# Two transformer blocks of each of two kinds on one core: rotary step of the windowed queries moved to GpSimd, maxima negated in the reduction, attention steps reordered

## The reference, cut to what matters

```python
proj = xn @ w_in[l]                       # 1824 columns
a_q, a_k, a_v, b_cq, b_ckv, b_kr, c_q, c_k, c_v = jnp.split(proj, IN_OFFSETS, axis=-1)
o_a = neighbourhood_attention(a_q, a_k, a_v, na_rpb[l])          # 4 heads, bias table na_rpb
o_b = latent_attention(b_cq, b_ckv, b_kr, ..., cos_r, sin_r)     # 6 heads, low-rank q and kv
o_c = window_gqa(c_q, c_k, c_v, swa_sink[l], cos, sin)           # 6 heads, 2 kv heads, sink logit
o = jnp.concatenate([rms_norm_2(o_a, ...), rms_norm_2(o_b, ...), rms_norm_2(o_c, ...)], axis=-1)
h = h + o @ w_out[l]
h = h + expert_choice_ffn(rms_norm_2(h, ffn_norm[l]), w_router[l], w_gate[l], w_up[l], w_down[l])

def apply_rope_2(x, cos, sin):
    x1, x2 = jnp.split(x, 2, axis=-1)
    return jnp.concatenate([x1 * c - x2 * s, x2 * c + x1 * s], axis=-1)
```

## Time and profile before

| | us |
|---|---|
| median of 3 runs | 2171.55 |
| lowest, highest | 2168.85, 2175.55 |
| the profiled execution, its own time | 2170.66 |
| its span, first to last instruction | 2169.4 |

### The profile page before, as it was taken

One profiled execution on the slowest core, in us unless ns is written; L12 is line 12 of the kernel. 1 busy time (PEld: TensorE's weight loads), 2 busy tenths in 40 slices (PEclk: granted clock), 3 DMA queues, 4 the chain that ended last, 5 costly groups with the idle time before them and its releaser, 6 DMA issues.

```text
span 2169.4 us, 31018 instructions
## 1 busy us (share of the span) xinstructions
PE 1861.0 (86%) x12840; PEld 1233.1 (57%) x12840; DVE 905.7 (42%) x1506; ACT 643.6 (30%) x1110; POOL 43.2 (2%) x46
## 2 busy tenths in 40 slices
PE   6999999999999999999898866676798997666666
PEld 3887888987888888988754311121275542121212
DVE  3675585655576576645762200000058520000002
ACT  3244235545244235534452100000055410000001
POOL 0001000000001000000000000000000000000000
PEclk8999999999999999999999987888899998888888
DMA  9565348456634344553749999999984799999997
GB/s 339 217 233 195 118 155 311 178 184 221 233 117 157 118 156 157 193 194 83 258 193 374 428 426 428 426 428 426 422 264 160 310 408 427 426 427 427 427 425 315
DMA packets 119749, 617.45 MB, mean 285 GB/s; under 512 B 18448, under 2 KB 21434, under 8 KB 86586
## 3 DMA queue, kind: packets, MB, share of 16 engines
q1 hardware_dynamic: 119034, 613.85, 71.6%
q10 hardware_dynamic: 576, 1.63, 0.2%
HBM read 614.40 MB, written 1.05 MB: 284 GB/s over the span
## 4 chain that ended last, share of the span: by engine, by line
PE 59%; DMA 27%; DVE 9%; ACT 2%; issue 1%; SPq 0%; POOL 0%; DVEq 0%; ACTq 0%
PE pb L704 57%; DMA ring<-in_w_up_dram 18%; DMA ar<-in_w_up_dram 4%; DMA x<-in_w_up_dram 3%; PE pb L707 2%; DVE ar L1654 2%; DVE ar L1646 1%; ACT ar L2443 1%; DMA ring<-in_ada_w_dram 1%; DMA ring<-in_w_down_dram 1%; DVE ar L1650 1%; DVE small L1662 1%; DVE x L1646 1%; ACT ar L2447 0%; DVE ar L1658 0%
## 5 line engine op out<-in xcount | busy, mean ns | idle before, releaser
L704 PE MATMUL pb<-ring,ar 128*32 128x512 f32 (+2 forms) x2144 | 408.5, 731 | 183.1 <-DMA ring<-in_w_up_dram 102.5
L704 PE MATMUL pb<-ar 64*64 64x64 f32 (+10 forms) x3680 | 418.9, 348 | 37.8 <-DMA ring<-in_w_up_dram 30.8
L2447 ACT COPY ar<-pb 128x512 f32<-128x512 f32 (+2 forms) x195 | 112.7, 578 | 910.1 <-PE pb L704 852.3
L1658 DVE COPY ar<-pb 128x512 f32<-128x512 f32 (+3 forms) x94 | 57.5, 612 | 723.2 <-PE pb L704 713.5
L704 PEld LDWEIGHTS pb<-ring,ar 128*32 128x32 f32 (+1 forms) x2144 | 106.4, 133 | 397.0 <-issue 383.0
L704 PEld LDWEIGHTS pb<-ar 64*64 64x64 f32 (+5 forms) x3680 | 217.9, 146 | 188.9 <-issue 165.9
L704 PE MATMUL pb<-hT,ring 128*128 128x256 f32 x1024 | 235.4, 386 | 0.4 <-ACT ar L2443 0.4
L704 PEld LDWEIGHTS pb<-hT,ring 128*128 128x128 f32 x1024 | 193.0, 192 | 33.6 <-issue 7.8
L1646 DVE TENSOR_TENSOR ws<-ring,ws 128x1024 fp32r<-128x1024 f32 x128 | 156.9, 1226 | 123.8 <-ACT ws L2447 122.0
L704 PE MATMUL pb<-hs,ws 128*128 128x256 f32 x1536 | 186.0, 283 | 3.7 <-ACT aux L2447 1.5
L704 PEld LDWEIGHTS pb<-hs,ws 128*128 128x128 f32 x1536 | 184.7, 192 | 5.6 <-ACT aux L2447 1.7
(11 more groups left out here) (177 smaller groups left out, 1647.8 us busy)
## 6 DMA issues: line engine op xcount, KB each, us to landing
ring<-in_w_down_dram SPq DMA_DIRECT2D x46, 2048.0 KB, 28.1
ring<-in_w_gate_dram SPq DMA_DIRECT2D x42, 2048.0 KB, 28.4
ring<-in_w_up_dram SPq DMA_DIRECT2D x42, 2048.0 KB, 23.6
ring<-in_w_mlp_dram SPq DMA_DIRECT2D x32, 2048.0 KB, 7.9
ring<-in_w_in_dram SPq DMA_DIRECT2D x27, 2048.0 KB, 9.2
ring<-in_ada_w_dram SPq DMA_DIRECT2D x24, 2048.0 KB, 8.0
ar<-in_w_gate_dram SPq DMA_DIRECT2D x12, 2048.0 KB, 27.7
ar<-in_w_up_dram SPq DMA_DIRECT2D x12, 2048.0 KB, 23.5
```

The lines of the kernel that those rows point to most:

```text
L704: return e.matmul(o, l, r, start=start, stop=stop)
L1658: return e.tensor_copy(o, i)
L2447: return e.copy(o, i)
```

## The change

- `l_rope` loses its `window` part on VectorE (five instructions for each of the two token halves). A new `l_rope` on GpSimd does the same rotation in six instructions for each half, with a scratch tile pT2[3]; `l_cT` on TensorE, and `c_copy 3` on ScalarE, which overwrites the scratch, wait for it.
- `m_max` takes the maximum with its sign turned in the reduction itself; the separate negation is gone. For the windowed heads the sink is folded in by a minimum with the negated sink (`no_sinks`, made once). The scale of the latent scores moves into the copy that makes mq.
- The steps of both windows stand in another sequence. Neighbourhood units and the latent path begin among the projection groups; `l_nab` comes after `x_lin 5` in window 0 and after `x_lin 1` in window 1, where it came after `x_lin 14`.
- `l_mkv` and `l_mT` get the waits that the new sequence needs. The lists of the first kind of block are only laid out anew.

```diff
@@ window_order, window 0
-        ("x_lin", 7), ("x_lin", 8), ("x_out", 1), ("x_lin", 9), ("l_aT",), ("x_lin", 10), ("x_lin", 11), ("x_lin", 12),
-        ("x_out", 2), ("x_lin", 13), ("x_lin", 14), ("l_nab",), ("x_lin", 15), ("l_lat",), ("x_out", 3), ("s_qk", 0),
+        ("x_lin", 0), ("x_lin", 1), ("x_lin", 2), ("x_lin", 3), ("x_out", 0), ("x_lin", 4), ("x_lin", 5), ("l_aT",),
+        ("l_nab",), ("x_lin", 6), ("x_lin", 7), ("s_qk", 0), ("m_max", 0), ("x_lin", 8), ("x_out", 1), ("x_lin", 9),
@@ window_order, window 1
-        ("x_out", 2), ("x_lin", 13), ("x_lin", 14), ("l_nab",), ("x_lin", 15), ("l_lat",), ("x_out", 3), ("l_cqT",),
+        ("x_lin", 0), ("x_lin", 1), ("l_nab",), ("x_lin", 2), ("x_lin", 3), ("x_out", 0), ("x_lin", 4), ("x_lin", 5),
@@ tensor, across / l_mkv / l_mT
-                    e.wait_ge(*V("cro", l))
+                    e.wait_ge(*G("cro", l))
...
+                e.wait_ge(*A("cqT", l, 1))
...
+                    e.wait_ge(*V("mkv", l, 1, 1))
+                    e.wait_ge(*V("k_rot", l))
@@ vector, l_rope
-                    m = rot(window, v4(P2[:, t, 1184:1696], 8), 8, 64, c64[:, t:t + 1, :], s64[:, t:t + 1, :])
-                    m.then_inc(*(V.up("cro", l) if t else step()))
@@ vector, m_max
-                reduce(st[:, 0:2], b3_, ALU.max).then_inc(*step())
+                own()
+                m = e.tensor_reduce(st[:, 0:2], b3_, AX.X, ALU.max, negate=True)
                 if u["sink"] is not None:
-                    ts(st[:, 0:2], st[:, 0:2], u["sink"][l], None, ALU.max).then_inc(*step())
-                ts(st[:, 2:4], st[:, 0:2], -sc, None, ALU.mult).then_inc(*V.up("nmax", l, s))
+                    m.then_inc(*step())
+                    m = ts(st[:, 0:2], st[:, 0:2], u["no_sink"][l], None, ALU.min)
+                m.then_inc(*V.up("nmax", l, s))
@@ pool, new l_rope (called after root(S("lat", 4), "lat", l))
+                e.wait_ge(*V("proj", "b", l, 3, 0))
+                e.wait_ge(*A("proj", "b", l, 3, 1))
+                for t in range(2):
+                    src = v4(P2[:, t, 1184:1696], 8)
+                    part = v4(pT2[3], 8)
+                    for h in range(2):
+                        tt(part[:, :, 32 * h:32 * h + 32], src[:, :, 32 - 32 * h:64 - 32 * h], bc(s64[:, t:t + 1, 32 * h:32 * h + 32], [128, 8, 32]),
+                           ALU.mult).then_inc(*G.up("step"))
...
+                    tt(q_to, src[:, 0:6, :].rearrange("p (v g) d -> p v g d", v=2), bc(c64[:, t:t + 1, :].unsqueeze(1), [128, 2, 3, 64]),
+                       ALU.mult).then_inc(*G.up("step"))
+                    tt(k_to, src[:, 6:8, :], bc(c64[:, t:t + 1, :], [128, 2, 64]), ALU.mult).then_inc(*G.up("step"))
+                    tt(q_to, q_to, part[:, 0:6, :].rearrange("p (v g) d -> p v g d", v=2), ALU.add).then_inc(*G.up("step"))
+                    m = tt(k_to, k_to, part[:, 6:8, :], ALU.add)
```

More of the change, by code:

```diff
@@ L85 @@
     "hidden": "relu relu2 h1_hi h1",
-    "latent": "lat_sq latent cro nab aqk cqT mq mkv mq_rot acT mT",
+    "latent": "lat_sq latent cro nab aqk cqT mq mkv mq_rot k_rot acT mT",
     "attn2": "s2 biased nmax exp2 scaled2 pT2 pv2 sq2 oT2",
@@ L246, in window_order @@
     return ((
-        ("x_lin", 0), ("x_lin", 1), ("x_lin", 2), ("x_lin", 3), ("x_lin", 4), ("x_out", 0), ("x_lin", 5), ("x_lin", 6),
-        ("x_lin", 7), ("x_lin", 8), ("x_out", 1), ("x_lin", 9), ("l_aT",), ("x_lin", 10), ("x_lin", 11), ("x_lin", 12),
-        ("x_out", 2), ("x_lin", 13), ("x_lin", 14), ("l_nab",), ("x_lin", 15), ("l_lat",), ("x_out", 3), ("s_qk", 0),
-        ("m_max", 0), ("e_exp", 0), ("e_exp", 1), ("l_cqT",), ("m_max", 1), ("e_exp", 2), ("s_qk", 2), ("l_rope",),
-        ("l_mq",), ("m_max", 2), ("n_norm", 0), ("l_mkv",), ("l_rot",), ("l_cT",), ("l_mT", 0), ("l_mT", 1), ("l_mT", 2),
@@ new lines, in window_order @@
+        ("x_lin", 0), ("x_lin", 1), ("x_lin", 2), ("x_lin", 3), ("x_out", 0), ("x_lin", 4), ("x_lin", 5), ("l_aT",),
+        ("l_nab",), ("x_lin", 6), ("x_lin", 7), ("s_qk", 0), ("m_max", 0), ("x_lin", 8), ("x_out", 1), ("x_lin", 9),
+        ("m_max", 1), ("x_lin", 10), ("e_exp", 0), ("n_norm", 0), ("x_lin", 11), ("x_out", 2), ("x_lin", 12), ("l_lat",),
+        ("e_exp", 1), ("s_qk", 2), ("x_lin", 13), ("x_lin", 14), ("l_cqT",), ("x_lin", 15), ("m_max", 2), ("m_max", 3),
+        ("x_out", 3), ("l_mkv",), ("l_mq",), ("l_rope",), ("n_norm", 1), ("e_exp", 2), ("t_turn", 0), ("c_copy", 0),
@@ new lines, in window_order @@
+        ("l_rot",), ("n_norm", 2), ("e_exp", 3), ("l_mT", 0), ("t_turn", 1), ("c_copy", 1), ("l_mT", 1), ("l_mT", 2),
+        ("s_qk", 4), ("l_mT", 3), ("t_turn", 2), ("e_exp", 4), ("m_max", 4), ("c_copy", 2), ("n_norm", 3), ("l_mT", 4),
+        ("l_mT", 5), ("s_qk", 5), ("l_cT",), ("t_turn", 3), ("m_max", 5), ("m_max", 6), ("n_norm", 4), ("n_norm", 5),
+        ("s_qk", 6), ("e_exp", 5), ("v_pv", 0), ("m_max", 7), ("s_qk", 7), ("v_pv", 1), ("s_qk", 8), ("c_copy", 3),
+        ("n_norm", 6), ("q_stat", 0), ("q_stat", 1), ("m_max", 8), ("t_turn", 4), ("s_qk", 9), ("r_root", 0),
@@ L594, in program @@
         sink = [sinks[:, 6 * l:6 * l + 6] for l in range(2)]
+        no_sinks = S("no_sinks", 12)
+        no_sink = [no_sinks[:, 6 * l:6 * l + 6] for l in range(2)]
         cin = v4(zone(ZST, 3120), 12)
@@ L665, in program @@
         for h in range(6):
-            units.append(dict(q=mT2[0:96, h, 0:256], k=mT2[0:96, h, 256:512], bias=None, scale=96 ** -0.5, sink=None,
+            units.append(dict(q=mT2[0:96, h, 0:256], k=mT2[0:96, h, 256:512], bias=None, scale=1.0, sink=None,
                               v=lambda kt, h=h: mv[:, kt, h, :], o=256 + 64 * h))
@@ L670, in program @@
             pp = slice(64 * kv, 64 * kv + 64)
-            units.append(dict(q=cT[pp, g, :], k=cT[pp, 3, :], bias=swa, scale=0.125, sink=[z[:, h:h + 1] for z in sink],
+            units.append(dict(q=cT[pp, g, :], k=cT[pp, 3, :], bias=swa, scale=0.125, sink=[z[:, h:h + 1] for z in sink], no_sink=[z[:, h:h + 1] for z in no_sink],
                               v=lambda kt, kv=kv: P2[:, kt, 1696 + 64 * kv:1760 + 64 * kv], o=640 + 64 * h))
@@ L1703, in lambdas @@
                 e.wait_ge(*D("rows"))
+                ts(no_sinks, sinks[:, :], -1.0, None, ALU.mult).then_inc(*step())
                 for l in range(2):
@@ L2285, in m_max @@
             def m_max(l, s):
-                u, st = units[s], S(f"u{s}", 10)
+                u, st = units[s], S(f"u{s}", 8)
                 b3_ = v4(ps("s2", l, s)[:, :], 2)
@@ L2860, in l_mq @@
                         e.wait_ge(*P("mq", l, t, s))
-                        copy(mq[:, t, 3 * s:3 * s + 3, :], v4(ps("mq", l, t, s)[:, 0:288], 3)).then_inc(*A.up("mq", l, t, s))
+                        act(mq[:, t, 3 * s:3 * s + 3, :], v4(ps("mq", l, t, s)[:, 0:288], 3), ACT.Copy, scale=96 ** -0.5).then_inc(*A.up("mq", l, t, s))
             def across(l, n):
@@ L2879, in e_exp @@
                 for t in range(2):
-                    m = act(e3[:, t, :], src[:, t, :], ACT.Exp, bias=st[:, 2 + t:3 + t], scale=sc, accum=st[:, 4 + t:5 + t])
+                    m = act(e3[:, t, :], src[:, t, :], ACT.Exp, bias=st[:, t:1 + t], scale=sc, accum=st[:, 2 + t:3 + t])
                     m.then_inc(*(A.up("exp2", l, s) if t and u["sink"] is None else step()))
                 if u["sink"] is not None:
-                    act(st[:, 8:10], st[:, 2:4], ACT.Exp, bias=u["sink"][l]).then_inc(*A.up("exp2", l, s))
+                    act(st[:, 6:8], st[:, 0:2], ACT.Exp, bias=u["sink"][l]).then_inc(*A.up("exp2", l, s))
             def c_copy(l, s):
@@ L2989, in pool @@
                 root(S("lat", 4), "lat", l)
+                l_rope(l)
                 for g in range(3):
```

193 lines of the change are left out of this document (105 added, 88 removed), and 17 rows, old and new, of the table k.

## The result

The changed kernel takes 2196.48 us (median; 2195.62 to 2199.38), the kernel before 2173.09 on the same chips (2168.85 to 2175.55). The ratio is 1.0106, with a 95% interval of 1.0091 to 1.0122: 23.4 us more. The forecast was 2197 and a slower kernel.

A forecast was written before the change was run, and what follows sets the result against it. TensorE bounds the windows and the weight stream the experts; 17.6 us in window 1 plus 7.8 in window 0 make 25.4, on 2170.66 giving 2196.1, by the median 2197 us, range 2179 to 2213.

The forecast's parts named there:

- The bound: Whole kernel: experts bound by the weight stream, both windows by TensorE; window delays move the end one to one.
- The pauses: TensorE waits for low weight parts behind l_nab: 11.3 us before x_lin 8 in window 0, 21.3 before x_lin 4 in window 1.
- What comes back: TensorE's idle time in the windows: 2.3 plus 3.7 us recovered in window 0, 6.2 in window 1.
- The clock: TensorE behind each pause: a granted clock of 0.50 costs 2.5 us.
- The sum: Both windows: 17.6 + 7.8 = 25.4 us slower (7.8 to 40.5), giving 2197 us.
- VectorE's relief: Negations and rotation off VectorE: 7.5 us less work a window, nothing more on the path.
- GpSimd: Rotation in each window: twelve instructions take 9 us (7 to 12), hidden before l_cT.
- VectorE as the bound: Rival, both windows: VectorE sets the pace, 23.5 us less work per window, net faster, 2157 us; chance 0.08.
- The port: Rival, both windows: GpSimd holds VectorE 9 us where TensorE waits for latent score copies; 43 us slower, 2215; chance 0.08.
- The third rival: Bias pieces land early at 5.8 us, 8 to 9 us idle time recovered per window: +7.8 and less; chance 0.04.

The follow-up runs named there:

- the run with one piece: The changed kernel with one of the 16 bias pieces loaded for each window, the other 15 DMAs left out: 2165.35 us, ratio 0.9966.
- the last experiment: Changed kernel with 8 larger bias DMAs, l_nab behind x_lin 8, m_max 0 behind x_lin 9, but rotation back on VectorE: 2173.35 us, ratio 0.9989.

## Why the prediction was right

**The bound.** Right. Both windows counted one to one, and the experts' length did not change: from the trigger on 433.4 against 433.1 us.

**The pauses.** Forecast 11.3 and 21.3, measured 12.64 and 22.00. The places, the releaser and the queue (VectorE's l_nab, then the low part) were as forecast. The changed kernel's window 0 began 1.43 us sooner (first piece at 1016.44, not 1017.87) and window 1 7.49 us later. With these shifts the forecast reads that TensorE stops at 1033.1 and 1605.9, and it did at 1032.81 and 1605.89; that it goes on at 1044.4 and 1627.2, and it did at 1045.45 and 1627.89. The last microsecond is the landing, 24 us forecast and some 25 measured after the first issue in window 0, 22.0 and 22.7 in window 1. The text of the prediction says "1616 less window 0's shift" where it must be plus: 1623.5, and l_nab started at 1624.22. Two more slips: 2171.55 + 40.5 gives an upper end of 2212, where the text has 2213, and the slack of 25 us that it gives VectorE is 29.6 and 35.2 by the earlier trace rows. Neither moves the forecast.

**What comes back.** Forecast 6.0 in window 0 and 6.2 in window 1; measured 6.9 and 7.9. The 4.9 us gap of window 0 is gone. The forecast's 6.0 holds 1.25 for half of the old slow stretch, which in the measured figures stands in the busy time; of idle time alone it had 4.75 and 6.2, so 3.8 us too little. The reason was half right: the experiment with l_nab early in the kernel before shows that a pause by itself gives back 1.2 to 1.5 us. The rest is what sequences and code save in any case, as the run with one piece shows (idle time of window 0 5.6 us, before 11.7).

**The clock.** Forecast 2.5 us behind each pause. The first products after them ran at half the granted clock, as window 0 and then window 1 show:

```profile
1045.45:1049.50 4.05, 4.05 (x10) 3.22 (x11) 2.60 (x3) 0.23 (x1) 0.00 (x0) 0.50 0.15 60
1627.90:1632.00 4.10, 4.10 (x10) 3.23 (x11) 1.98 (x2) 0.29 (x1) 0.00 (x0) 0.50 0.00 0
```

That is 2.0 us in each; in window 1 the low clock lasted on to about 1633.2, 0.6 us more of loss. TensorE's busy time grew by 3.98 and 3.00, although the slow stretch of the kernel before was gone from window 0. The rest lies in a place I had not looked at: the routing at the window's end. In window 0:

```profile
1149.00:1155.00 6.00, 5.76 (x19) 4.42 (x20) 2.29 (x11) 3.70 (x8) 0.00 (x0) 0.50 0.32 135
```

There TensorE has small products (128x16 and 128x256) around VectorE's top-k search. The clock was low in the changed kernel from about 1148.5 to 1155.2 and from 1158.8 to 1162.1, in window 1 from 1745.9 to 1749.4, and in the profile before at none of these places. The section at the end shows that the same sequence can run through it either way, so I don't put it down to the change. Behind the pauses alone the clock cost 2.0 and 2.6 us, 4.6 against a forecast of 5.0; that the whole busy time grew by 7.0 has another reason, which the forecast did not hold.

**The sum.** Measured in the profiled executions: pauses 34.6, less 14.8 of idle time recovered, and 7.0 of longer busy time, make 26.8. Window 0 began 1.4 us sooner and the experts of block 0 were 0.8 us shorter, which nothing in the change explains; with 0.3 behind the trigger 24.9. The forecast was 32.6 - 12.2 + 5.0 = 25.4. The three terms are 2.0, 2.6 and 2.0 us off and offset one another in part. By the medians the loss was 23.4 us and not 25.4: the kernel before read 2173.09 beside the changed one, and 2171.55 in the runs that the forecast started from. So the agreement to the last microseconds (2197 against 2196.5) is luck.

**VectorE's relief.** Forecast "nothing more on the path", 7.5 us less work in a window. Its busy time fell by 5.1 and 5.0. The negations give 2.7 of it, the rotation only 2.4 of its 5.0, since VectorE loses the rest beside GpSimd. That nothing of it lies on the path was wrong for the new sequence: the last experiment puts the rotation at 7.9 us for both windows, in a version whose data come in time. What it is worth in the changed kernel itself was not run. The sum held nevertheless, presumably because this gain is inside the idle time recovered.

**GpSimd.** Forecast 9 us for twelve instructions, hidden. Here they are in window 0 (four lines, twelve instructions):

```profile
1069.88 2.80 POOL L2985 TENSOR_TENSOR ar<-ar,c 128x256 f32<-128x256 f32 x4 [6.47 <-DVE ar L1656]
1072.76 1.58 POOL L2985 TENSOR_TENSOR ar<-ar 128x384 f32<-128x384 f32 x2
1074.41 3.24 POOL L2985 TENSOR_TENSOR ar<-ar,c 128x256 f32<-128x256 f32 x4
1077.73 1.53 POOL L2985 TENSOR_TENSOR ar<-ar 128x384 f32<-128x384 f32 x2
```

9.2 us (the prediction's 7.1 by elements is 7.0, its 9 was right), and no wait of TensorE in the windows of the changed kernel is ended by GpSimd.

**The rivals.** VectorE as the bound fell: with one piece only, and 5.0 us of pause left, the changed kernel gains 8.2 us, not the 2 x 23.5 = 47 that the rival takes for granted. The port was real and small. The rows of `l_rot` in window 1, before and then changed:

```profile
1643.54 2.71 DVE L1646 TENSOR_TENSOR ar<-ar 128x192 f32<-128x192 f32 x8
```

```profile
1674.13 3.94 DVE L1652 TENSOR_TENSOR ar<-ar 128x192 f32<-128x192 f32 x8
```

1.2 us more for eight instructions with two SBUF inputs, the first half of them beside GpSimd (until 1676.49), where the copies from PSUM in front of them, beside GpSimd too, take 3.31 as before. In all VectorE loses 2.6 us a window, not the 9 that the prediction set as the most; in time the rotation on GpSimd was a gain (the last experiment). The Trainium skill, "SBUF — State Buffer", section "Who interferes with whom", says that a VectorE instruction with at most one SBUF input, outside the modes that use both ports, doesn't contend with GpSimd; the copies agree, 3.31 us with and without it. The third rival (pieces early, idle time back) fell by its first half: the last pieces landed 11.8 and 9.8 us after their issue, far from the median of 5.8. Its price was stated with a slip, since 7.8 us lies just outside of 0.3%.

## What to carry to other kernels

A step that waits for a late load blocks every step behind it on its engine, also those that have nothing to do with the load; before moving one forward, compare the landing of its last piece with the time at which the engine will get there, and count what the other engines need from behind it. Look at the number of DMAs when a load is late: eight in place of sixteen let l_nab start 9.6 and 7.5 us sooner here. And judge a change by its parts and by their sum: one misplaced step hid a gain of 8 to 10 us.

## What the hardware showed that was not expected

- **A DMA's issue time.** 64 KB in 256 rows and 96 KB in 384 rows of 256 bytes both took SyncE 0.82 to 0.88 us, and the last piece landed 9.3 and 9.5 us after its issue against 9.8 to 12.6.
- **The clock in the routing.** The same sequence ran through it at different clocks. Window 1 of the kernel before near its end, and the same place of that kernel with the eight DMAs, where only the load and l_nab differ and both are long over:

```profile
1724.00:1736.00 12.00, 9.97 (x73) 6.37 (x72) 7.57 (x20) 2.69 (x3) 0.00 (x0) 1.00 0.62 236
```

```profile
1724.00:1737.00 13.00, 12.08 (x40) 10.00 (x41) 5.58 (x19) 3.50 (x5) 0.00 (x0) 0.50 0.66 257
```

  TensorE's busy time of that window was 129.71 in the one and 135.54 us in the other, and its length 142.33 and 146.81. Where the clock fell in the routing of the other profiles, it was low for 3 to 14 us. This may be much of the spread of the kernel before, whose executions lie between 2169 and 2183 us apart from one of 2190; what decides it, no run here shows.
- **A short pause and a long one cost the clock alike.** Behind 12.6 and 22.0 us it stayed at half for 4.1 and 5.3 us, behind the 4.9 us gap for some 4.9.
